# Dilated-attention stage: key splits, feature splits and sums re-ordered, GpSimd's key residues given to VectorE

## The reference, cut to what matters

```python
u = rmsnorm(h) @ w_in                     # 4242 columns: conv, sparse and dilated branches, gates
y_b = nsa(...)                            # 6 heads: compressed keys, selected blocks, window; gated sum
y_c = dilated_mixer(d_q, d_k, d_v)        # 6 heads in 3 pairs: dilation 1, 4 and 16
h = h + concat(y_a, y_b, y_c) @ w_out
h = h + sigmoid(h @ w_ple_gate) * (p @ w_ple_proj)   # p: 512 tokens x 256 features
return rmsnorm(h)
```

## Time and profile before

| | us |
|---|---|
| executions timed | 1324.33, 1327.9, 1329.0 |
| their median | 1327.9 |
| the profiled execution's own time | 1324.35 |
| its span, first to last instruction | 1322.3 |
| TensorE busy | 1297.4 (98% of the span) |
| VectorE busy | 755.1 (57%) |
| ScalarE busy | 520.9 (39%) |
| GpSimd busy | 33.9 (3%) |
| mean granted TensorE clock | 0.998 |

### The profile page before, as it was taken

How to read it: one execution, slowest core, us unless ns; L and a number is a source line. 1 busy time by engine, 2 the same in 40 slices (tenths; PEclk the granted TensorE clock), 3 DMA queues, 4 the chain that set the end, 5 groups by cost and what they waited for, 6 DMA issues and landing times.

```text
span 1322.3 us, 16209 instructions
## 1 busy us (share of the span) xinstructions
PE 1297.4 (98%) x6163; PEld 1073.2 (81%) x6163; DVE 755.1 (57%) x1048; ACT 520.9 (39%) x753; POOL 33.9 (3%) x31
## 2 busy tenths in 40 slices
PE   7999999999999999999999999999999999999998
PEld 7788888888888777788888888888888878888777
DVE  6844535444447775564544444445858388886554
ACT  6442232323334555432323223333323255565434
POOL 0510000000000000000000000000000000011000
PEclk9999999999999999999999999999999999999999
DMA  5343333222332111233232322233524221113211
GB/s 190 96 127 95 95 95 95 79 87 88 107 100 78 50 41 65 64 96 97 93 103 87 113 74 84 92 107 103 170 75 159 64 64 33 49 48 128 96 64 64
DMA packets 120887, 119.54 MB, mean 90 GB/s; under 512 B 13500, under 2 KB 117896, under 8 KB 120584
## 3 DMA queue, kind: packets, MB, share of 16 engines
q1 hardware_dynamic: 120784, 118.89, 28.5%
q10 hardware_dynamic: 56, 0.01, 0.0%
HBM read 114.70 MB, written 4.19 MB: 90 GB/s over the span
## 4 chain that ended last, share of the span: by engine, by line
PE 88%; DVE 7%; ACT 3%; issue 2%; DMA 0%; DVEq 0%; SPq 0%; ACTq 0%
PE psum L1926 26%; PE psum L1928 26%; PE psum L1927 26%; PE psum L2133 1%; PE psum L2110 1%; ACT w_hi L658 1%; PE psum L2295 1%; DVE w_lo L1167 1%; PE psum L2267 1%; PE psum L2281 1%; PE psum L2120 1%; PE psum L1964 1%; PE psum L2429 1%; DVE du L1505 0%; DVE xg_lo L1227 0%
## 5 line engine op out<-in xcount | busy, mean ns | idle before, releaser
L1926 PE MATMUL psum<-xg_hi,w_hi 128*128 128x512 f32 x1088 | 433.0, 398 | 1.4 <-DVE w_lo L1167 0.9
L1928 PE MATMUL psum<-xg_hi,w_lo 128*128 128x512 f32 x1088 | 424.2, 390 | 0.0
L1927 PE MATMUL psum<-xg_lo,w_hi 128*128 128x512 f32 x1088 | 424.2, 390 | 0.0
L1926 PEld LDWEIGHTS psum<-xg_hi,w_hi 128*128 128x128 f32 x1088 | 204.9, 188 | 44.4 <-issue 1.5
L1928 PEld LDWEIGHTS psum<-xg_hi,w_lo 128*128 128x128 f32 x1088 | 204.5, 188 | 43.6
L1927 PEld LDWEIGHTS psum<-xg_lo,w_hi 128*128 128x128 f32 x1088 | 204.8, 188 | 40.8 <-issue 1.2
L1301 DVE TENSOR_TENSOR w_lo<-w_raw,w_hi 128x2048 fp32r<-128x2048 f32 x40 | 91.8, 2294 | 145.6 <-ACT w_hi L751 145.6
L1328 DVE TENSOR_TENSOR w_lo<-w_raw,w_hi 128x2048 fp32r<-128x2048 f32 x32 | 73.3, 2292 | 115.6 <-ACT w_hi L777 115.6
L1926 PE MATMUL psum<-act_hi,w_hi 128*128 128x512 f32 x352 | 137.2, 390 | 0.0
L1927 PE MATMUL psum<-act_lo,w_hi 128*128 128x512 f32 x352 | 137.0, 389 | 0.0
L1928 PE MATMUL psum<-act_hi,w_lo 128*128 128x512 f32 x352 | 137.0, 389 | 0.0
(11 more groups left out here) (374 smaller groups left out, 1601.7 us busy)
## 6 DMA issues: line engine op xcount, KB each, us to landing
w_raw<-in_ffn_w_gate SPq DMA_DIRECT2D x22, 1024.0 KB, 5.1
w_raw<-in_ffn_w_up SPq DMA_DIRECT2D x22, 1024.0 KB, 5.1
w_raw<-in_w_in SPq DMA_DIRECT2D x16, 1024.0 KB, 5.4
w_raw<-in_ffn_w_down SPq DMA_DIRECT2D x16, 768.0 KB, 4.8
w_raw<-in_ffn_w_down SPq DMA_DIRECT2D x16, 640.0 KB, 4.5
w_raw<-in_mla_w_o SPq DMA_DIRECT2D x4, 1024.0 KB, 5.1
w_raw<-in_w_out SPq DMA_DIRECT2D x4, 1024.0 KB, 5.0
w_raw<-in_w_ple_gate SPq DMA_DIRECT2D x4, 1024.0 KB, 4.9
```

The costliest lines, as they stand in the source:

```text
L1926: pe.matmul(o, wh, xh, start=start, stop=False, skip_group_check=True)
L1927: pe.matmul(o, wh, xl, start=False, stop=False, skip_group_check=True)
L1928: return pe.matmul(o, wl, xh, start=False, stop=stop, skip_group_check=True)
```

## The change: what it does

- The transposes of the two halves of `p_cmp` move from step 3 to steps 5 and 9, the second into bank 4 in place of bank 6, after the projection tile there has been evacuated. The last multiplication of the compressed softmax moves from the end of `w_in` to VectorE's step 3.
- The features `p` come already transposed from memory (`features_2`, laid out on the host). TensorE's two `features` groups go, and the splits read `du` in place of bank 4.
- The six key halves of the second heads go from GpSimd to VectorE: (1,1) at steps 27 and 29, (1,2) and (1,0) in `dilated`. (1,1) lives in `d_key`, which lies over `squares`. The second half of the first heads' last key tile moves from step 45 to step 48.
- ScalarE's split of the ple_proj weights moves from step 47 to step 46; its order at the start of `dilated` changes.
- VectorE's order in `dilated` changes: `dilated_max(1)` and the last query residue ahead of the features; the split of the first w_out unit in thirds around `spread(1)`; that of the second ahead of the gates.

```diff
+        key_mem = ExitStack()
+        d_key = sb("d_key", [P, 2, T], F32R, key_mem)
+        key_mem.close()
...
-            return bank[(7, 6)[g]]
+            return bank[(7, 4)[g]]
+        C_STEPS = (5, 9)
...
-            sp.dma_start(p_tok, a["p_2"][0, 0].rearrange("(i p) f -> p i f", p=P)).then_inc(sem("p_loaded"), 16)
+            sp.dma_start(pT, a["features_2"]).then_inc(sem("p_loaded"), 16)
...
-            for n, g in enumerate((1, 2, 0)):
-                hi, lo = d_keys(1, g)
-                pool.wait_ge(sem("dk_hi"), 6 + 2 * n + 2)
-                for e in range(2):
-                    pool.tensor_tensor(lo[64 * e:64 * e + 64, :], du[64:128, 3 + g, :], hi[64:128, :].bitcast(F32), ALU.subtract).then_inc(sem("dk1_lo"), 1)
...
# ScalarE, nsa
-                    if s == 3:
-                        for g in range(2):
-                            act.wait_ge(sem("c_turned"), g + 1)
...
+                    if s in C_STEPS:
+                        g = C_STEPS.index(s)
+                        act.wait_ge(sem("c_turned"), g + 1)
...
+                    if s == 26:
+                        act.wait_ge(sem("u_free"), KINDS.index("dk") + 2)
+                        act.wait_ge(sem("c_turned"), 2)
+                        keys_hi(1, 1)
...
-                    if step == 2 and w % 2 == 1 and w < NT - W_MAIN - 1:
+                    if step == 2 and w % 2 == 1 and w <= NT - W_MAIN:
                         split_hi(FIRST["w_in"] + (W_MAIN - 1 + w) // 2 + 2)
-                    if s == 47:
-                        split_hi(FIRST["ple_proj"])
...
# ScalarE, dilated
-                keys_hi(1, 1)
+                keys_hi(1, 2)
                 turned_hi(46)
                 softmax_exp(0)
+                turned_hi(47)
+                dilated_query(5)
                 features_hi(0)
-                turned_hi(47)
-                keys_hi(1, 2)
+                softmax_exp(1)
                 features_hi(1)
-                dilated_query(5)
-                softmax_exp(1)
...
# VectorE, compress
+                if t == W_MAIN:
                     dve.wait_ge(st, 7)
                     dve.tensor_tensor(pc, pc, wide(3), ALU.mult).then_inc(*mark("cmp_probs"))
...
# VectorE, nsa
                     if s == 3:
+                        compress(W_MAIN)
+                    if s - 1 in C_STEPS:
+                        g = C_STEPS.index(s - 1)
...
-                    if s in (31, 35, 45):
-                        keys_lo((31, 35, 45).index(s))
+                    if s in (27, 29):
+                        keys_lo(0, ((s - 27) // 2,))
+                    if s in (31, 35):
+                        keys_lo((s - 27) // 4, (0, 1))
+                    if s in (45, 48):
+                        keys_lo(3, ((s - 45) // 3,))
...
# VectorE, dilated
                 split_lo(FIRST["ple_proj"], 0)
+                turned_lo(47)
+                keys_lo(4, (0, 1))
+                dilated_max(1)
+                dilated_query_lo(5)
                 features_lo(0)
-                turned_lo(47)
-                dilated_max(1)
-                features_lo(1)
-                dilated_query_lo(5)
                 split_lo(FIRST["ple_proj"], 1)
                 split_lo(FIRST["ple_proj"], 2)
+                features_lo(1)
                 sparse_sum(5)
                 spread(0)
                 dilated_max(2)
+                keys_lo(5, (0, 1))
                 embedding(0)
...
-                split_lo(n_out)
-                y_lo(2)
+                split_lo(n_out, 0)
                 spread(1)
+                split_lo(n_out, 1)
                 embedding(3)
                 factors(1)
                 rows(2)
+                split_lo(n_out, 2)
+                y_lo(2)
+                embedding(4)
                 y_lo(3)
-                embedding(4)
...
+                split_lo(n_out + 1)
                 gate(0, 1)
                 gate(1, 2)
                 gate(2, 0)
-                split_lo(n_out + 1)
...
# TensorE
-                    if s == 1:
-                        pe.wait_ge(sem("c_lo"), 2)
...
-                        pe.wait_ge(*(sem("n_sum"), h) if h else (sem("c_lo"), 2))
+                        pe.wait_ge(*(sem("n_sum"), h) if h else (sem("c_lo"), 1))
+                        if h == 3:
+                            pe.wait_ge(sem("c_lo"), 2)
...
+                        if s == 12:
+                            pe.wait_ge(sem("c_lo"), 2)
...
+                        if s in C_STEPS:
+                            g = C_STEPS.index(s)
+                            pe.wait_ge(*((sem("u_free"), W_MAIN + 2) if g else at("cmp_probs")))
...
-                features(0)
                 dilated_scores(1)
                 turn(47)
                 values(45)
                 values(46)
-                features(1)
                 values(47)
...
-                pe.wait_ge(*((sem("dk_lo"), 2), (sem("dk_lo"), 6), (sem("dk1_lo"), 4), (sem("dk1_lo"), 6))[x])
+                pe.wait_ge(*((sem("dk_lo"), 4), (sem("dk_lo"), 8), (sem("dk_lo"), 10), (sem("dk_lo"), 12))[x])
```

More of the change, by code:

```diff
@@ L1646, in add_halves, with keys_lo @@
                 dve.tensor_tensor(dst, dst, total[r, :], ALU.mult).then_inc(done, 1)
-            def keys_lo(g):
-                hi, lo = d_keys(0, g)
-                dve.wait_ge(sem("dk_hi"), 2 * g + 2)
-                for e in range(2):
-                    dve.tensor_tensor(lo[64 * e:64 * e + 64, :], du[0:64, 3 + g, :], hi[0:64, :].bitcast(F32), ALU.subtract).then_inc(sem("dk_lo"), 1)
+            def keys_lo(n, halves):
+                j, g = ((1, 1), (0, 0), (0, 1), (0, 2), (1, 2), (1, 0))[n]
+                r = slice(64 * j, 64 * j + 64)
+                hi, lo = d_keys(j, g)
+                dve.wait_ge(sem("dk_hi"), 2 * n + 2)
+                for e in halves:
+                    dve.tensor_tensor(lo[64 * e:64 * e + 64, :], du[r, 3 + g, :], hi[r, :].bitcast(F32), ALU.subtract).then_inc(sem("dk_lo"), 1)
             sums = [0]
@@ L1716, in nsa @@
                     if s == 3:
-                        for g in range(2):
-                            dve.wait_ge(sem("c_hi"), g + 1)
-                            dve.tensor_tensor(ptc_lo[:, g, :], c_bank(g)[0:96, :], ptc_hi[:, g, :].bitcast(F32), ALU.subtract).then_inc(sem("c_lo"), 1)
+                        compress(W_MAIN)
+                    if s - 1 in C_STEPS:
+                        g = C_STEPS.index(s - 1)
+                        dve.wait_ge(sem("c_hi"), g + 1)
+                        dve.tensor_tensor(ptc_lo[:, g, :], c_bank(g)[0:96, :], ptc_hi[:, g, :].bitcast(F32), ALU.subtract).then_inc(sem("c_lo"), 1)
                     w, step = divmod(s, 4)
@@ L2319, in nsa @@
                         scores(s)
-                        if s == 3:
-                            pe.wait_ge(*at("cmp_probs"))
-                            for g in range(2):
-                                for i in range(NB):
-                                    c = (g * NB + i) * 96
-                                    mm = pe.transpose(c_bank(g)[0:96, i * P:(i + 1) * P], p_cmp[:, c:c + 96], ident[:, :])
-                                mm.then_inc(sem("c_turned"), 1)
+                        if s in C_STEPS:
+                            g = C_STEPS.index(s)
+                            pe.wait_ge(*((sem("u_free"), W_MAIN + 2) if g else at("cmp_probs")))
+                            for i in range(NB):
+                                c = (g * NB + i) * 96
+                                mm = pe.transpose(c_bank(g)[0:96, i * P:(i + 1) * P], p_cmp[:, c:c + 96], ident[:, :])
+                            mm.then_inc(sem("c_turned"), 1)
                     if 0 <= s - 3 < len(NSTEP):
@@ L2353, in dilated_values @@
                 mm.then_inc(sem("dv_turned"), 1)
-            def features(m):
-                pe.wait_ge(sem("p_loaded"), 16)
-                pe.wait_ge(*(sem("p_lo_ready"), 1) if m else (sem("u_free"), NT))
-                for i in range(NB):
-                    mm = pe.transpose(bank[4][:, i * P:(i + 1) * P], p_tok[:, i, m * P:(m + 1) * P], ident[:, :])
-                mm.then_inc(sem("p_turned"), 1)
             def dilated_scores(x):
@@ L2553, in _, with constants @@
             tail()
-def constants():
+def constants(features):
     import numpy as np
@@ L2593 @@
     arrays, aps = {}, {}
-    for name, v in list(inputs.items()) + list(constants().items()):
+    kept = {name: v for name, v in inputs.items() if name != "p_2"}
+    for name, v in list(kept.items()) + list(constants(inputs["p_2"]).items()):
         v = np.ascontiguousarray(v)
```

17 lines of the change are left out of this document (10 added, 7 removed).

## The result

The changed kernel took 1318.82 us (median of 6 executions, 1318.1 to 1319.5), the kernel before 1326.76 us beside it (6 executions, 1324.33 to 1329.0): a ratio of 0.994, 95% interval [0.9923, 0.9957]. It is faster by 0.6%. The profiled execution took 1318.1 us with a span of 1316.3 us, against 1324.35 and 1322.3 us before: the span is 6.0 us shorter.

A forecast was written before the change was run, and what follows sets the result against it. TensorE, busy 1297.4 of 1322.3 us, was taken as the bound, with VectorE close to it in the step loop. Terms 0.1 + 1.3 + 1.5 + 1.5 + 1.1 = 5.5 us off the median 1327.9 gave 1322.4 us; range 1317 to 1326.5.

The forecast's parts named there:

- opening, to behind step 9: Steps 3 to 9: `values(0)` 1.6 us earlier, part given back at step 9; 0.8 us gained, bounds 0 and 2.0.
- key half in step 29: Step 29 has no VectorE gap, so the half delays row maximum, ScalarE and TensorE at 1139.16: 0.7 us lost.
- from there to `embedding(1)`: Step 47 to `embedding(1)`: local gain 2.1 us, less 0.7 for two embedding waits and 0.1 for roundings: 1.3.
- `spread(1)` in front of two thirds: Ahead of `cross(1)`: only one third of the split precedes `spread(1)`, so the 1.34 us wait goes; 1.5 us gained.
- clock after `cross(1)`: Transposes and matmuls from 1211: without the wait ahead of `cross(1)` the low clock goes; 1.5 us, bounds 0 and 1.5.
- w_out, second unit: Third w_out part: the second unit's split no longer stands behind the gates, so the wait goes; 1.1 us gained.
- Step 47 and the features: Waits of 0.7 and 0.6 us and 0.8 of transposes go, less 0.25 at `values(47)`: local gain about 1.8 us.
- forecast of 2.1 us: Local gain at `dilated_scores(2)`, to start at 1189.45, not 1191.57, with VectorE making the (1,2) pair; bounds 1 us either way.
- VectorE as the bound: Rival: six halves add 4.2 us to VectorE and 3.1 lands on TensorE; gain 2.4, time 1325.5 us; chance 0.18.
- the one from the profiled execution to the median: Gain of 5.5 us set against the median 1327.9, 3.55 above the profiled execution: 1322.4 us, not 1318.85.
- clock rival: Dilated stage: clock falls all the same, at the old place or after the wait at 1187.45; 1323.9 us; chance 0.17.
- slower case: The new wait takes the clock down at 1189, low to the end of `embedding(7)`; 8.9 us slower, 1336.8; chance 0.03.

The follow-up runs named there:

- u1: Changed kernel with the opening undone: both halves of `p_cmp` transposed at step 3, the last multiplication back in `w_in`; 1320.78 us.
- v2: Changed kernel with the second half of key (1,1) made at step 43, not 29; 1318.75 us.
- u3: Changed kernel with the second w_out unit's split behind the three gates again; 1320.22 us.
- u2: Changed kernel with the first w_out unit's split in one piece ahead of `spread(1)` again; 1320.42 us.
- v1: Changed kernel with the (1,2) and (1,0) residues back on GpSimd, ScalarE keeping its new order; 1316.73 us.
- w1: Changed kernel with eight unused transposes put where the features' were, four behind `values(44)`, four ahead of `values(47)`; 1319.29 us.
- u4: Changed kernel with VectorE's last query residue ahead of the maxima of pass 1; 1318.65 us.
- b1: The kernel before, unchanged, in a second profiled execution; 1324.11 us.
- v3: Changed kernel with residues (1,2) and (1,0) back on GpSimd and the second half of key (1,1) at step 43; 1315.78 us.

## Why the prediction was right, and where it was not

| step | gain forecast, us | gain in the first profile, us |
|---|---|---|
| opening, to behind step 9 | 0.8 | 0.89 |
| key half in step 29 | -0.7 | -0.93 |
| from there to `embedding(1)` | 1.3 | 1.40 |
| `spread(1)` in front of two thirds | 1.5 | 1.46 |
| clock after `cross(1)` | 1.5 | 1.72 |
| w_out, second unit | 1.1 | 1.09 |
| sum | 5.5 | 5.6, and 0.4 outside these stretches |

In the first profile the sum came out term by term, two of them for a reason that is partly another. Undoing one part each gives 0.84 for the opening (u1), 0.88 for step 29 (v2), 1.2 for w_out (u3) and 1.7 for the clock (u2). For `spread(1)` u2 gives only 0.8 of the 1.5. I had put the whole wait down to the split of 2.28 us; 0.6 of it was `y_lo(2)` behind the split, which the change moved as well (u2). The forecast for an execution like the profiled one was 1318.85 us; it took 1318.1.

- **The waits.** `values(0)` waited 0.43 us for `ptc_lo` (0.6 forecast), step 9 0.24 (0.4), `dilated_scores(2)` 1.91 for `q_st` (1.5 to 2.5). That the 2.12 us of the kernel before were GpSimd's pair and not the exponentials the trace names fits v1: with the pair done early the wait is 0.46 us. The pair alone held TensorE for the last 1.2 of the 2.12 us only, since the query residue too was not done until 1190.29 (1189.60 plus 0.69); so with the pair alone out of the way TensorE would, by these rows, still have waited until about 1190.4.
- **Step 29** was under-sized: 0.7 by the length of the half, 0.87 on TensorE in step 32 (the running gain falls from 0.83 at its scores to nothing at its projection). The chain over `neg_max`, ScalarE and `dv_kept` was right, v2 takes it away.
- **Step 47 and the features.** The wait of 0.71 us is gone; the two groups of transposes counted in full in my sum. w1 shows that this was right for one group only: put back, they cost 0.41 us and not 0.8. That the whole came out is thus in part luck. The forecast of 2.1 us came out (2.4 from step 32 to `dilated_scores(2)`) because the time there was set by VectorE's list, which I had also followed, and not by TensorE's gain in front of it.
- **VectorE as the bound** was given 0.18 as a loss of 3.1 us. It is the bound, from 1185 to 1192 us (u4), but what had been there before, GpSimd's late pairs, was worse. The part of the change that silences GpSimd cost time: v1 keeps ScalarE's new order, gives two pairs back, and needs 1.6 us less than the changed kernel from the first scores to the end, both at full clock in this stage (258.41 and 260.00 us). What helped, by GpSimd's start 5.6 us earlier than before (1182.62, not 1188.26), was the early hi part; no run changes ScalarE's order alone.

**The step that failed is the one from the profiled execution to the median.** I wrote that the median shown lay 3.55 us above the profiled one "without any difference in code", and carried these 3.55 us over to the changed kernel: 1322.4. By the table above they are low clock, and the change takes much of it away. Why it does is argued, not shown: the old kernel has two long waits among short instructions in this stage and the changed one has one, and a fall cost 1.6 us there and 0.6 to 0.9 here. At the same clock of 0.999 the kernels are 4.4 us apart; their medians over all executions are 6.8 us apart. My term for the clock, one stretch of 1.5 us, was right for one profile and too small for the median, and the changed kernel's median came out 3.6 us below the forecast, inside the range of 1317 to 1326.5. Of the 3.6 us, 2.4 are gain (7.9 between the medians of the result, where 5.5 was forecast), and 1.1 is that the kernel before had a median of 1326.76 over six executions and not the 1327.9 of three. For the same reason "within 0.5%" got 0.59 and "faster" 0.38, and 0.6% was measured.

The clock rival had said that the fall would come all the same, at the old place or after the new wait, and got 0.17 because the old 2.12 us wait had passed at 1.00. One profile could not show that: a second (b1) has the fall just there. Ten of the 13 executions of the changed kernel are below 0.999. By the Trainium skill's page "TensorE: Matmul & The Clock Gate", Part 1, recent activity is what lifts the rate. The traces agree in that each fall seen in this stage stands behind a wait (of 0.75 to 2.12 us), and they add that behind the same wait it comes in some executions and not in others. The slower case, low clock to the end of the stage, did not come: each fall in these profiles lies within a stretch of 8 us.

What stays open: where the low clock of the old kernel's executions at 0.994 and 0.995 lies, since none of them was profiled, and what decides whether a wait is followed by a fall.

## What to carry to other kernels

Follow the lists of the engines instruction by instruction and the sum can hold within some tenths, as here; then undo the parts one by one, since a sum can hold with the gain booked on the wrong edit. A wait ahead of TensorE is slack for TensorE's own work only if the releaser's list does not itself hang on that work. Before a median is explained by an offset, sort the executions by granted clock: where they spread over more than a fraction of a per cent, short waits among short matmuls can cost more than their own length (2.5 us for a wait of 0.8 in u2). An engine that delivers late should first get its input early, and only then be relieved of the work.

## What the runs showed of the hardware that I had not expected

- Whether TensorE's clock falls after a wait of 1.3 to 2.1 us differs between executions of one kernel. A fall cost 0.6 to 1.7 us, and in the kernel before it stood at another place in each of the two profiles. In u2 one came after a wait of only 0.75 us, ahead of matmuls with 16 and 64 columns.
- Beside GpSimd's subtractions of 64x512, VectorE's two additions of 128x32 took 1.39 us instead of 0.30 and its residue of 128x768 took 1.73 instead of 0.95 (v3), while in the kernel before the query residue at 1189.60 kept its 0.69 us in the middle of GpSimd's second pair. The starts of the single subtractions sort this. GpSimd in the kernel before, then in v3:

```profile
1188.26 1.28 POOL L644 TENSOR_TENSOR xg_lo<-du,xg_hi 64x512 fp32r<-64x512 f32 x1 [0.97 <-ACT xg_hi L950]
...
1189.62 1.79 POOL L644 TENSOR_TENSOR xg_lo<-du,xg_hi 64x512 fp32r<-64x512 f32 x1
```

```profile
1182.61 1.28 POOL L649 TENSOR_TENSOR xg_lo<-du,xg_hi 64x512 fp32r<-64x512 f32 x1
...
1191.06 1.26 POOL L649 TENSOR_TENSOR xg_lo<-du,xg_hi 64x512 fp32r<-64x512 f32 x1 [7.17 <-ACT xg_hi L956]
```

In each case the instruction that started first kept its length, and the other ended as if it had begun only when the first was done. The query residue started 0.02 us ahead of GpSimd's second subtraction, and it was that one which took 1.79 us and not 1.28; the thirds of ple_proj, begun at 1190.32, ended 1.42 us after it (1191.41). In v3 the 128x768 residue ended 0.82 us after GpSimd's at 1182.61 did (1183.89), and the additions 0.16 us after GpSimd's at 1191.06 did (1192.32). VectorE's instructions that read PSUM kept their length beside GpSimd in these traces (in the kernel before, the feature residue at 1186.75 took its usual 0.69 us, though GpSimd's first pair ran from 1184.05 to 1187.30). No run was made to test this reading.
